# A two-layer hybrid trunk with a routed expert layer: two more slab places free at the trunk's end, and shorter token fetches

## The reference, cut to what matters

```python
x = x + hybrid_mixer(x, mem, ...)                  # ends in merged @ w_out
h = rms_norm(x, ffn_norm_g[1])
logits = h @ w_router                              # 256 x 8
top_val, top_idx = lax.top_k(logits, 2)
combine = sum(one_hot(top_idx) * softmax(top_val)) # 256 x 8, two non-zero in a row
for e in range(8):
    gt, up = split(h @ w_gate_up[e])               # 1024 x 7168
    x = x + combine[:, e:e+1] * ((silu(gt) * up) @ w_down[e])   # 3584 x 1024
```

## Time and profile before

| | us |
|---|---|
| median of three runs | 1584.41 (1583.47 to 1584.98) |
| the profiled execution | 1584.69 |
| its span | 1582.9 |
| TensorE busy | 1536.5 (97%) |
| VectorE busy | 521.0 (33%) |
| ScalarE busy | 457.0 (29%) |
| GpSimd busy | 90.3 (6%) |
| moved by DMA | 485.63 MB, mean 307 GB/s |

### The profile page before, as it was taken

The page is one execution under the profiler, slowest core; times in us unless marked ns, Lnnn a source line. Parts: engine busy times, 40 slices in busy tenths (PEclk is TensorE's granted clock), DMA queues, the critical chain, the costliest instruction groups (busy, mean ns, idle before and its releaser), DMA issues.

```text
span 1582.9 us, 32047 instructions
## 1 busy us (share of the span) xinstructions
PE 1536.5 (97%) x14130; PEld 965.2 (61%) x14130; DVE 521.0 (33%) x619; ACT 457.0 (29%) x598; POOL 90.3 (6%) x128
## 2 busy tenths in 40 slices
PE   8999999999999999999999999999999999999876
PEld 7788888788888888887345353454533533544223
DVE  5755575655567556665100101001010010010000
ACT  5557654544455666552000000000000000000000
POOL 5211100000002111000000000000000000000000
PEclk9999999999999999998999999999999999999999
DMA  8555454766665554787999999999999999999995
GB/s 274 179 158 153 145 179 154 226 186 191 182 185 188 152 180 140 249 308 293 419 408 372 419 417 418 419 417 418 418 419 418 418 418 417 417 418 418 418 419 246
DMA packets 110241, 485.63 MB, mean 307 GB/s; under 512 B 13024, under 2 KB 15136, under 8 KB 67104
## 3 DMA queue, kind: packets, MB, share of 16 engines
q1 hardware_dynamic: 107056, 474.68, 78.9%
q0 software_dynamic: 3056, 8.99, 1.6%
HBM read 481.53 MB, written 2.10 MB: 306 GB/s over the span
## 4 chain that ended last, share of the span: by engine, by line
PE 84%; DMA 8%; SPq 2%; DVE 2%; POOL 2%; issue 1%; ACT 0%; DVEq 0%; POOLq 0%
PE pa L2036 27%; PE ps L2036 18%; PE pa L1907 12%; PE pa L1909 12%; PE pa L1908 12%; DMA exp_raw<-in_moe_slabs 7%; SPq L584 2%; PE ps L2314 1%; DVE w_lo L1229 1%; DMA w_raw<-in_w_mem_kv 1%; POOL hrs L724 1%; POOL head_gains L653 0%; PE ps L2284 0%; PE ps L1834 0%; DVE hs L1784 0%
## 5 line engine op out<-in xcount | busy, mean ns | idle before, releaser
L2036 PE MATMUL pa<-exp_raw,xf 128*32 128x512 f32 (+1 forms) x5120 | 502.0, 543 | 21.6 <-DMA exp_raw<-in_moe_slabs 11.9
L2036 PEld LDWEIGHTS pa<-exp_raw,xf 128*32 128x32 f32 x5120 | 161.0, 110 | 320.4 <-issue 254.8
L1229 DVE TENSOR_TENSOR w_lo<-w_raw,w_hi 128x1024 fp32r<-128x1024 f32 x226 | 274.2, 1232 | 121.9 <-ACT w_hi L859 112.9
L859 ACT ACTIVATE w_hi<-w_raw 128x1024 fp32r<-128x1024 f32 (+1 forms) x228 | 236.9, 1053 | 146.5 <-PE pa L1909 145.0
L2036 PE MATMUL ps<-exp_raw,hf 128*32 128x256 f32 x4480 | 250.7, 380 | 9.8 <-DMA exp_raw<-in_moe_slabs 9.8
L1907 PE MATMUL pa<-w_hi,r 128*128 128x512 f32 x600 | 239.7, 399 | 1.4 <-DVE r L1264 1.3
L1909 PE MATMUL pa<-w_hi,r 128*128 128x512 f32 x600 | 234.0, 390 | 0.0
L1908 PE MATMUL pa<-w_lo,r 128*128 128x512 f32 x600 | 233.9, 390 | 0.0
L2036 PEld LDWEIGHTS ps<-exp_raw,hf 128*32 128x32 f32 x4480 | 143.9, 110 | 117.0 <-issue 16.3
L1784 DVE TENSOR_TENSOR hs<-pa,hs 128x768 f32<-128x768 f32 (+3 forms) x32 | 23.7, 742 | 348.5 <-ACT hs L1191 348.5
L1907 PEld LDWEIGHTS pa<-w_hi,r 128*128 128x128 f32 x600 | 112.7, 188 | 28.6 <-issue 3.2
(11 more groups left out here) (274 smaller groups left out, 863.0 us busy)
## 6 DMA issues: line engine op xcount, KB each, us to landing
exp_raw<-in_moe_slabs SPq DMA_DIRECT2D x336, 1024.0 KB, 26.8
w_raw<-in_w_in SPq DMA_DIRECT2D x104, 512.0 KB, 4.3
w_raw<-in_ff_w_gate_up SPq DMA_DIRECT2D x44, 512.0 KB, 4.6
w_raw<-in_ff_w_down SPq DMA_DIRECT2D x22, 512.0 KB, 3.9
w_raw<-in_w_mem_kv SPq DMA_DIRECT2D x16, 512.0 KB, 5.2
w_raw<-in_w_out SPq DMA_DIRECT2D x16, 512.0 KB, 4.3
w_raw<-in_w_br_sb SPq DMA_DIRECT2D x8, 512.0 KB, 3.7
w_raw<-in_w_br_gla SPq DMA_DIRECT2D x8, 512.0 KB, 4.2
```

The lines of the kernel that those rows point to most:

```text
L859: act.activation(dst, raw, ACT.Copy).then_inc(hi_ready, 1)
L1229: dve.tensor_tensor(dst, raw, hi.bitcast(F32), ALU.subtract)\
L2036: return pe.matmul(dst, a, b, start=start, stop=stop, skip_group_check=True)
```

## The change

The pieces of memory: the gain moves ahead of `w_raw`; `w_hi` and `w_lo` become one buffer `w_split`, in which the high and low half of a slab lie side by side, so a place of the ring lies over one split pair. `PLACES` has a new order. The router's tokens (`route_x`) lie on two raw places instead of on a branch's output; the last two squares go to `w_raw[0]` instead of `gates`, and ScalarE waits for the last low half before the first of them. So slab by slab the waits ahead of the issue are:

| slab | before | after |
|---|---|---|
| 11 | last low half | last merge |
| 12 | (behind 11) | (behind 11) |
| 13 | last slab used | last low half |
| 14 | (behind 13) | use of the slab five before the end |
| 15 to 17 | (behind 13) | last slab used (at 15) |
| 18 | norm done | (behind 15) |
| 19 | (behind 18) | norm done |
| 20 | router's logits | router's logits |

The fetch in slot `i` takes as many rows as the next slot has places: 64 in slot 0, then 96, 64, 96, 96, 64, 64 and 64. GpSimd's loop over the slots is written out for slots 1 to 6.

```diff
-            w_hi = early("w_hi", [P, SPLIT, SLAB], F32R)
-            w_lo = early("w_lo", [P, SPLIT, SLAB], F32R)
+            w_split = early("w_split", [P, SPLIT, 2, SLAB], F32R)
...
-        PLACES = (0, 1, 2, 3, 4, 20, 5, 6, 7, 17, 18, 9, 10, 11, 12, 13, 14, 15, 8, 16, 19)
+        FREE_PAIR = (PRE - SPLIT) % SPLIT
+        LATE_PAIRS = tuple(12 + n for n in range(SPLIT) if n != FREE_PAIR)
+        PLACES = (0, 1, 2, 3, 4, 20, 5, 6, 7, 17, 18, 8, 19, 11, 12 + FREE_PAIR) + LATE_PAIRS + (9, 10)
...
-        route_x = exp_raw[:, 19, :].rearrange("p (t k c) -> p t k c", t=NT, k=KT)
+        route_x = exp_raw[:, 10, :].rearrange("p (t k c) -> p t k c", t=NT, k=KT)
+        w_hi, w_lo = w_split[:, :, 0, :], w_split[:, :, 1, :]
...
                     elif j == 11:
+                        sp.wait_ge(merge_step, NT * BRANCHES * LAYERS)
+                    elif j == 13:
                         sp.wait_ge(lo_ready, PRE)
-                    elif j == 13:
+                    elif j == 14:
+                        sp.wait_ge(slab_used, PRE - SPLIT + 1)
+                    elif j == 15:
                         sp.wait_ge(slab_used, PRE)
-                    elif j == 18:
+                    elif j == 19:
                         sp.wait_ge(norm_done, NT * 3 * LAYERS)
...
-            def fetch_tokens(i):
+            def fetch_tokens(i, blocks_next):
+                n = blocks_next * LANE
...
-                    out=xg_tok[:, :], out_offset=None, in_=h_rows[:, :],
-                    in_offset=bass.IndirectOffsetOnAxis(ap=token_of[:, 0:1], axis=0),
+                    out=xg_tok[0:n, :], out_offset=None, in_=h_rows[:, :],
+                    in_offset=bass.IndirectOffsetOnAxis(ap=token_of[0:n, 0:1], axis=0),
...
-            fetch_tokens(0)
+            fetch_tokens(0, blocks_of(1))
...
-            with pool.Fori(1, slots) as i:
-                fetch_tokens(i)
+            for i in range(1, len(BLOCKS_AT)):
+                fetch_tokens(i, blocks_of(i + 1))
+            with pool.Fori(len(BLOCKS_AT), slots) as i:
+                fetch_tokens(i, FEW_BLOCKS)
...
                     act.wait_ge(taken["rows"], residual("out", p.layer, 0))
-                    square(xs, 0)
+                    if last_out(p):
+                        act.wait_ge(lo_ready, PRE)
+                        square(xs, 0, w_raw[:, 0, :])
+                    else:
+                        square(xs, 0)
...
-            square(xs, 1)
+            square(xs, 1, w_raw[:, 0, :])
```

More of the change, by code:

```diff
@@ L220, in trunk @@
             gates = early("gates", [P, NT, DM])
+            gain = early("gain", [P, DM])
             w_raw = early("w_raw", [P, RAW, SLAB])
-            w_hi = early("w_hi", [P, SPLIT, SLAB], F32R)
-            w_lo = early("w_lo", [P, SPLIT, SLAB], F32R)
-            gain = early("gain", [P, DM])
+            w_split = early("w_split", [P, SPLIT, 2, SLAB], F32R)
             r1 = early("r1", [P, 8192], F32R)
@@ L875, in visit, with square @@
                 return visits
-            def square(src, t):
-                act.activation(gates[:, t, :], src[:, t, :], ACT.Square, accum_out=nms[:, t:t + 1])\
-                    .then_inc(norm_sq, 1)
+            def square(src, t, squares=None):
+                act.activation(gates[:, t, :] if squares is None else squares, src[:, t, :], ACT.Square,
+                               accum_out=nms[:, t:t + 1]).then_inc(norm_sq, 1)
             turns = 0
```

## The result

The changed kernel takes 1587.39 us (median of 18 runs, 1586.39 to 1592.27), the kernel before 1583.89 (18 runs, 1582.31 to 1584.98). The ratio is 1.0024, 95% interval 1.0017 to 1.0030: 3.5 to 3.8 us slower, small but clear. The forecast was 3.6 us faster. The profiled execution has a span of 1586.2 us, 3.3 more than before.

A forecast was written before the change was run, and what follows sets the result against it. TensorE was taken to bound the kernel to about 868 us, then transfer bytes at 418 GB/s to the last slab. Terms 0 + 0 + 0 + 3.6 = 3.6 us off the median 1584.41 gave 1580.8 us, range 1577.0 to 1584.2.

The forecast's parts named there:

- the term of the fetches: Experts' part: fetches 1 to 7 leave out 352 rows, 1.442 MB, worth 3.6 us off, with ends 3.4 and 4.1.
- rival C: Fetches: rows dealt to engines by place, so only one half is relieved; 1584.4 or 1577.2 us; chance 0.10.
- D: Rival on fetches: fewer rows go to fewer engines; 1586.4 us on 8 engines, 1597.5 on 4; chance 0.06.
- Their own sign, a tail of another length: End of transfers: under C or D the half-rate tail's length would change by several microseconds.
- B: Rival on 815 to 870 us: no full ring there, so the two-slab lead of 5.0 us survives; 1575.8 us; chance 0.08.
- the trunk's end: Before the first expert slot: the experts' first matmul stays at 745 us.
- the added wait on ScalarE: Before the last two squares: low half done at 719.5 us, square at 725.2; 5.7 us of cover, cost 0.
- the two slabs at 0 with the full ring: Before 868 us: two slabs issued earlier, 5.0 us of transfer, lost once all places are full; 0, bounds 0 to 2.0.
- the unrolled loop at 0: GpSimd's fetch loop as six unrolled bodies: it waits 743.6 us for VectorE's token numbers in all, so 0.
- bytes after 868 us are worth their transfer time: From about 868 us to the last slab the queue never empties, so only bytes count, at 418 GB/s.

## Why the prediction was wrong

The step that failed is the term of the fetches, put at 3.6 us saved: "Fetches 1 to 7 leave out ... 352 rows, 1.442 MB", "I take 3.6, with 3.4 and 4.1 as ends". The bytes were right (7.28 MB on the queue, 7.3 forecast); the step took for granted that a packet costs what it cost in a 128-row gather. Bounds from below were missing: I had none for a gather that slows its neighbours. Measured, the three 96-row and four 64-row fetches cost 3.5 us (the kernel with nothing else), a miss of 7.1 on this term, which is the whole error (1580.8 against 1587.4, with the median of before 0.5 lower in more runs). So the last slab was issued at 1547.75 us, 3.2 later, where the forecast had it 3.6 earlier.

What the runs show in its place: rows written to one neighbouring half of the partitions slow the stream beside them. With the same rows and the same bytes, partitions 0 to 63 cost 2.8 us, partitions 64 to 127 cost 3.3, every second partition gives 4.35 back; 128 rows as two halves one after the other cost 13.6. So it isn't the number of rows, nor which rows are read. The best account I have is a write side that is loaded unevenly, and that is argued. Two places of the Trainium skill fit it. SBUF — State Buffer, section Door 1: The DMA port swizzle, says that partitions 0 to 63 reach only 8 of the 16 ports and 64 to 127 the other 8; by its table every second partition reaches all 16. The dips agree, 395 and 394 against 418 GB/s. The Trainium skill, DMA: Bandwidth & Descriptors, section Why a DMA increments its semaphore by 16 and not by 1, makes it 16 engines for 64 rows. Half of them would then write into the other half's ports, which the slabs' packets use too. That four in five of the slabs' packets beside such a fetch are slow, and not half of them, says that more than half of the engines are held up. I had cited the number of engines and the assignment of a 128-partition transfer in rival C, and drawn from them only who saves how much, never that an engine's packets could block another's. That these ports are where the packets queue is not shown: no record here names a port.

Rivals C and D went by the same blind spot. Both share out a fixed price, and then a full queue loses no rate; but the total fell by 16 to 27 GB/s while the engines were busy. Their own sign, a tail of another length, didn't come either: eight engines run alone for 13.4 us before and 13.7 after, and for 13.1 to 13.7 us with 64 rows in the low half, in the high half or spread. Had rows gone to the engines by place, or to eight engines only, a fetch of 64 would have spared half of the engines 7 x 8 x 0.164 = 9.2 us and the others nothing. D's sum for eight engines, 1586.4, lies near the measured 1587.4 for the wrong reason. B is refuted: with the slabs alone the time stayed.

What held: the trunk's end (the added wait on ScalarE is covered: the last low half is done at 720.0 us, the square starts at 725.7 and runs 1.06 us as before), the two slabs at 0 with the full ring, the unrolled loop at 0, and that bytes after 868 us are worth their transfer time, provided that they are spread: 4.35 measured for 4.39 worked out.

A second idea of mine, that the late half of the engines was the low partitions', fell by the tails of the two kernels that leave out empty places. Open is why eight engines end some 13 us after the others. The instruction queue's packets are a candidate. After 868 us there are 70 of them in the trace of before, 75 us in all, and behind nearly each one a slab's packet takes 0.8 us or so in place of 0.32, 34 us more in sum. If all of that fell on eight engines it would be 13.6 us each; but no record names an engine, and it was not tried.

## What to carry to other kernels

A gather beside a saturated stream is priced by what it does to the stream: compare the total rate in a window around one with that of a window beside it, and don't price it by its bytes. A share of 1.01 stood at 418 GB/s and at 394. Spread few rows over all 128 partitions (the copy out of PSUM has to step by two as well, and cost nothing that could be seen), or leave rows out of the full-width form by an index beyond the last row. And before crediting an earlier transfer, look for the next place where the ring is full.

## What the runs showed of the hardware that was not expected

- A gather of 64 rows into partitions 0 to 63, or 64 to 127, beside a stream of 418 GB/s costs about 1.0 us of that rate, its own bytes counted in, where leaving 64 rows out saves 0.63 us. As two halves, 128 rows lose 1.8 to 1.9 us a fetch.
- The loss falls on other transfers' packets in flight: the stream's 8 KB packets took 427 to 453 ns while such a gather of 64 rows ran, 316 and 317 beside one of 128 rows or to every second partition.
- A gather into every second partition runs at full rate, and rows with an index beyond the bound move no data (8.99 MB fell to 6.61 with the packet count at 3056).
- In the kernel before, eight of the sixteen transfer engines finish 13 us before the others, after some 690 us at full rate.
